# All hyena filter spectra in one opening stage, and the context's convolution behind both latent orders

## The chip, the cores and the metric

The kernel runs on one core of a Trainium2 chip. The metric is device time of one execution, in microseconds (us). The core has five engines with a queue of instructions each: TensorE (PE, matrix multiply, with its weight loads listed as PEld), VectorE (DVE), ScalarE (ACT), GpSimd (POOL) and SyncE (SP). SP and POOL issue the transfers (DMA) between HBM and the on-chip memories, SBUF and PSUM (where matmuls write). Engines wait for each other on semaphores. "Granted clock" is the share of TensorE's full clock that the profile shows: 1.00 is the level of 2.4 GHz, 0.50 that of 1.2 GHz.

## The reference

A two-layer backbone over 1024 latent tokens and 256 context tokens of width 1024. In each layer one input projection feeds three mixers side by side (hyena, retention, latent attention), then come an output projection and an MLP. The change touches the opening and the hyena mixer. A hyena mixer convolves 256 channels twice (two "orders") with a filter as long as the sequence, through Fourier transforms. The filter comes from a small network of the position alone, so its spectrum depends on the layer's weights and the length, and on no token:

```
def hyena_filter_spectrum(L, w1, b1, sin_freq, w2, b2, w3):
    ...
    z = jnp.concatenate([t, jnp.cos(ang), -jnp.sin(ang)], axis=-1)
    h = jnp.sin(sin_freq[0] * (z @ w1 + b1))
    h = jnp.sin(sin_freq[1] * (h @ w2 + b2))
    h = (h @ w3).reshape(L, 2, HY_ORDER, HY_WIDTH)
    ...
    h = h * jnp.exp(-t[:, :, None, None] * deltas)
    fwd, bwd = h[:, 0], h[:, 1]
    kern = jnp.concatenate([(fwd[0] + bwd[0])[None], fwd[1:], jnp.zeros_like(fwd[:1]), bwd[1:][::-1]], axis=0)
    kern = kern / jnp.sum(jnp.abs(kern), axis=0, keepdims=True)
    return jnp.fft.rfft(kern, axis=0)

def long_conv(z, kf, bias):
    ...
    y = jnp.fft.irfft(jnp.fft.rfft(zf, n=2 * L, axis=1) * kf, n=2 * L, axis=1)[:, :L]
    return (y + zf * bias).astype(z.dtype)

def hyena_mixer(u, conv_w, conv_b, w1, b1, sin_freq, w2, b2, w3, bias):
    ...
    u = short_conv(u, conv_w, conv_b)
    x1, x2, v = jnp.split(u, 3, axis=-1)
    ...
    z = x1 * long_conv(v, kf[:, 0], bias[0])
    return x2 * long_conv(z, kf[:, 1], bias[1])
```

The first layer runs the mixer on latent and context tokens, the second on latent tokens only. The modulation of a layer is silu(c) @ w_ada + b_ada for both conditions.

## The kernel before, in words

The program is a chain of blocks; every engine finishes a block before any starts the next. Within a block each engine's instructions run in the order in which the code writes them.

**Opening.** `phase_start` (L158) loads two condition vectors. `phase_ada` (L185) multiplies them with the first third of w_ada in eight chunks of 1 MB ("chunks" below), through a ring of six buffers: 8 matmuls of 256 columns each (L247), two small transposes (L239), a bias add on DVE. SP then loads x (5 MB) and ACT takes its square sums (L155).

**Hyena.** `phase_hyena(kit, l, s)` runs three times: layer 0 latent (s=0), layer 0 context (s=1), layer 1 latent. Each run has:
- a block (L1605) that loads, runs the filter network (two sines, on 64 partitions) and the short convolution of V, and starts the transfer of the transform tables on POOL's queue (L1585, 12 MB for the latent length);
- for each order o a block (L1691) that computes the filter's taps (L1704: full fp32 matmuls with 64 contraction rows), multiplies them with a decay (L1759), splits them into a high and a low part (L1723 on ACT, L1771 on DVE), sums absolute values (L1726, L1773, L1747) for the norm (L1717, L1781, L1782), and turns z by transposes (L1714);
- a block (L1798) that transforms the filter ("K forward": four tiles kt of 48 matmuls of 256 columns), multiplies it by the norm (L1872, L1898 to L1904), transforms z ("z forward", the same size, f0 to f3 below), forms the products of the two for each kt (DVE L1913 to L1925, POOL L1879 to L1885, ACT L1861 to L1865), transforms back (b0 to b3, each 24 matmuls of 512 columns), and computes the outputs (L1930, L1932). DVE also runs the three-tap short convolution of that order's gate there (`conv`, L1590 to L1593). After order 1 SP stores the result (L1806).

Each product of two fp32 matrices is done as three fp32r matmuls (L143 to L145), high×high, high×low, low×high. The stage behind the latest hyena run is the output projection, whose first load on SP (L1990) shows where hyena ended.

Of the kernel before, what the change touches and what calls it, by code (L numbers as in the profile page):

```python
# [19 lines left out]
F32 = mybir.dt.float32  # L20
# [5 lines left out]
P = 128  # L26
# [69 lines left out]
class Kit:  # L96


    def __init__(self, nc, ctx, io):
        self.nc = nc  # L100
        self.ctx = ctx
        self.io = io
        self.base = ((nc.sbuf_base + 31) // 32) * 32
        self.big = self.base + SMALL
        self.signals = {}
        self.placed = {}
# [6 lines left out]
    def sig(self, name, step=1):  # L113
        if name not in self.signals:
            self.signals[name] = Signal(self.nc, self.ctx, name, step)
        return self.signals[name]

# [40 lines left out]
def phase_start(kit):  # L158

    nc, io, s = kit.nc, kit.io, kit  # L160
    loaded = kit.sig("start_loaded", 16)
    loaded.plan(["ident", "c0", "c1"])
    craw = kit.at("craw", [P, 2, KT], 120)
    with nc.Block() as block:
        @block.sync
        def _(sp):
            sp.dma_start(kit.ident[:], io["ident"]).then_inc(loaded.sem, 16)
            sp.dma_start(craw[:, 0, :], io["c"][0].rearrange("(p j) -> p j", j=KT)).then_inc(loaded.sem, 16)
            sp.dma_start(craw[:, 1, :], io["c_ctx"].rearrange("(p j) -> p j", j=KT)).then_inc(loaded.sem, 16)
# [12 lines left out]
ADA_W = 256


def phase_ada(kit):  # L185


    nc, io, ps = kit.nc, kit.io, kit.ps
    n_chunks = 2 * D // ADA_W
    ring = 6  # L190
    w = kit.at("ada_w", [P, ring, KT, ADA_W], 122)
    bias = kit.at("ada_bias", [2, 2 * D], 0)
    row = kit.at("ada_row", [2, 2 * D], 24)
# [6 lines left out]
    w_in = [kit.sig(f"ada_w_in{s}", 16) for s in range(ring)]  # L200
    for s in range(ring):
        w_in[s].plan([c for c in range(n_chunks) if c % ring == s])
    small_in, summed, added = kit.sig("ada_small_in", 16), kit.sig("ada_summed"), kit.sig("ada_added")
    turned, mod_ready = kit.sig("ada_turned"), kit.sig("ada_mod_ready")
    small_in.plan(range(3))
    for s in (summed, added, turned, mod_ready):
        s.plan(range(n_chunks))
    w_dram = io["w_ada"][0].rearrange("(p j) n -> p j n", j=KT)
    with nc.Block() as block:
        @block.sync  # L210
        def _(sp):
            for cond in range(2):
                sp.dma_start(bias[cond:cond + 1, :], io["b_ada"][0:1, 0:2 * D]).then_inc(small_in.sem, 16)
            sp.dma_start(gain[:, :, :], io["norm_g"][0]).then_inc(small_in.sem, 16)
            for c in range(n_chunks):
                if c >= ring:
                    sp.wait_ge(summed.sem, summed[c - ring])
                sp.dma_start(w[:, c % ring, :, :], w_dram[:, :, c * ADA_W:(c + 1) * ADA_W]).then_inc(w_in[c % ring].sem, 16)

            for i in range(2):  # L220
                sp.dma_start(x[:, 4 * i:4 * i + 4, :],
                             io["x"][0, 512 * i:512 * i + 512].rearrange("(t p) n -> p t n", p=P)).then_inc(x_in[i].sem, 16)
            sp.dma_start(x[:, 8:10, :], io["ctx"][0].rearrange("(t p) n -> p t n", p=P)).then_inc(x_in[2].sem, 16)
            for i in range(3):
                sp.wait_ge(x_in[i].sem, x_in[i][0])

        @block.scalar
        def _(act):
            for t in range(ALL_TILES):
                act.wait_ge(x_in[t // 4].sem, x_in[t // 4][0])  # L230
                square_sum(kit, act, squared, t, 4)

        @block.tensor
        def _(pe):
            def turn(c):
                pe.wait_ge(added.sem, added[c])
                for h in range(ADA_W // P):
                    at = c * ADA_W + h * P
                    last = pe.transpose(ps[:, 2 + c % 2, 2 * h:2 * h + 2], row[:, at:at + P], kit.ident[0:2, 0:2])  # L239
                last.then_inc(turned.sem, 1)  # L240

            for c in range(n_chunks):
                pe.wait_ge(w_in[c % ring].sem, w_in[c % ring][c])
                if c >= 2:
                    pe.wait_ge(added.sem, added[c - 2])
                for j in range(KT):
                    last = pe.matmul(ps[0:2, c % 2, 0:ADA_W], kit.cond[:, j, :], w[:, c % ring, j, :],  # L247
                                     start=(j == 0), stop=(j == KT - 1))
                last.then_inc(summed.sem, 1)
                if c:  # L250
                    turn(c - 1)
            turn(n_chunks - 1)

        @block.vector
        def _(dve):
            def mod(c):
                dve.wait_ge(turned.sem, turned[c])
                for h in range(ADA_W // P):
                    t = c * (ADA_W // P) + h
                    last = dve.tensor_copy(kit.mod[:, t, :], ps[:, 2 + c % 2, 2 * h:2 * h + 2])  # L260
                last.then_inc(mod_ready.sem, 1)

            dve.wait_ge(small_in.sem, small_in[2])
            for c in range(n_chunks):
                dve.wait_ge(summed.sem, summed[c])
                cols = slice(c * ADA_W, (c + 1) * ADA_W)
                dve.tensor_tensor(row[:, cols], ps[0:2, c % 2, 0:ADA_W], bias[:, cols], ALU.add).then_inc(added.sem, 1)
                if c:
                    mod(c - 1)
            mod(n_chunks - 1)  # L270
            dve.wait_ge(mod_ready.sem, mod_ready[n_chunks - 1])
            modulation_factor(kit, dve, gain, 0)

# [341 lines left out]
def phase_in(kit, l):  # L615
# [22 lines left out]
    stored = [kit.sig(f"in_stored{s}", 16) for s in range(2)]  # L638
# [904 lines left out]
def phase_hyena(kit, l, s):  # L1543

# [16 lines left out]
    z = kit.at(f"hy_z{s}", [P, 2, length], 160)
    h2 = kit.at(f"hy_h2{s}", [HY_FFN, length], 168)
    w3 = kit.at("hy_w3", [HY_FFN, 2, 2 * W], 172)
    w3_raw = kit.at("hy_w3_raw", [HY_FFN, 4 * W], 176)
    feat = kit.at(f"hy_feat{s}", [HY_EMB, length], 112)
    v_in = kit.at(f"hy_v_in{s}", [P, 2, length + 2], 117)
    w1, w2 = kit.at("hy_w1", [HY_EMB, HY_FFN], 116), kit.at("hy_w2", [HY_FFN, HY_FFN], 116.25)
    cols = kit.at("hy_cols", [HY_FFN, 4], 116.5)
    arg, rnd = kit.at(f"hy_arg{s}", [HY_FFN, length], 96), kit.at(f"hy_rnd{s}", [HY_FFN, length], 100)
    h1 = kit.at(f"hy_h1{s}", [HY_FFN, length], 104)  # L1570
# [3 lines left out]
    xg = kit.at(f"hy_gate{s}", [P, 2, length], 194)  # L1574
    knorm = kit.at("hy_knorm", [P, W], 202)
    decay, ksum = kit.at(f"hy_decay{s}", [P, 2 * K, W], 96), kit.at("hy_ksum", [P, W], 203)
    pmf, pabs = kit.at("hy_pmf", [P, 2, 2, W], 176), kit.at("hy_pabs", [P, 2, 2, W], 184)
    u_in = [kit.at(f"hy_u_in{s}", [P, length + 2], kb) for kb in (104, 188)]
    n_chunk = max(1, length // 512)
    CH = min(512, length)  # L1580

    def tables(pool, which):
        for i in which:
            for a in range(2):
                pool.dma_start(tabs[i][a][:], io[f"hy_tab{s}"][i, a]).then_inc(tab_in.sem, 16)  # L1585

    def conv(dve, out, u, part):

        w = kit.hy_conv[:, part, :]
# [862 lines left out]
```

## Time and profile before

| | us |
|---|---|
| three runs: lowest, median, highest | 4262.32, 4266.14, 4268.31 |
| the profiled execution's span | 4261.7 |
| TensorE busy in it | 3720.1 |
| opening, 0 to 49.9 | 49.9 |
| hyena layer 0, latent, 943.4 to 1198.1 | 254.7 |
| hyena layer 0, context, 1198.1 to 1286.9 | 88.8 |
| hyena layer 1, latent, 3137.2 to 3396.3 | 259.2 |

The span is one execution on the profiler's clock; the runs are timed apart from it. The stages' limits are where SP issues a stage's first transfer, which it can only do when all engines have left the block before. The four stages make up 652.6 us of the span. A row of the timeline gives start and duration in us, engine, line, operation, tiles, count, and in brackets how long the engine sat idle before it and what released it.

### The profile page before, as it was taken

How to read it: one execution, taken by the hardware profiler on the slowest of the kernel's cores; microseconds unless marked ns; L12 is line 12 of the kernel's file. 1: busy time of each engine (PE TensorE's matmuls, PEld its weight loads, DVE VectorE, ACT ScalarE, POOL GpSimd, SP SyncE). 2: the span in 40 equal slices, each digit the busy share in tenths (PEclk: the TensorE clock that was granted, in tenths of full speed). 3: DMA queues.
4: the chain of work that ended last, by engine and by line, in shares of the span. 5: the costliest groups of instructions: out<-in, count | busy, mean ns of one | idle time of the engine just before them, and what ended most of it. 6: DMA issues, size and time to landing. Idle time of an engine off the chain costs nothing. (4 is left out here: it accounts for less than half of the span.)

```text
span 4261.7 us, 54579 instructions
## 1 busy us (share of the span) xinstructions
PE 3720.1 (87%) x20116; PEld 3116.5 (73%) x20116; DVE 2267.7 (53%) x3970; ACT 1415.5 (33%) x2841; POOL 1306.3 (31%) x1182
## 2 busy tenths in 40 slices
PE   6997688877847899999999897698968788999998
PEld 4897577766625688888888697577847767888886
DVE  4853566656663344444444752576766625445454
ACT  3112466651111422222223312466741123222222
POOL 1211011123331155555554211011123313545454
PEclk8998799997868899999999898799978899999999
DMA  5530000012013111111110630000040122111111
GB/s 188 192 110 3 28 1 13 1 54 112 20 43 141 50 40 39 39 39 39 34 35 10 203 121 4 25 1 11 6 157 20 45 95 69 59 39 52 47 49 54
DMA packets 145678, 243.97 MB, mean 57 GB/s; under 512 B 9480, under 2 KB 113689, under 8 KB 141915
## 3 DMA queue, kind: packets, MB, share of 16 engines
q1 hardware_dynamic: 138108, 208.57, 14.8%
q0 software_dynamic: 7392, 33.03, 2.1%
q8 instruction: 111, 1.82, 0.2%
q14 instruction: 67, 0.54, 0.0%
HBM read 215.60 MB, written 25.99 MB: 57 GB/s over the span
## 5 line engine op out<-in xcount | busy, mean ns | idle before, releaser
L2242 POOL TENSOR_TENSOR x<-x,mlp_tmp 128x512 f32<-128x512 f32 x576 | 785.5, 1396 | 805.9 <-DVE mlp_tmp L2223 800.8
L2223 DVE TENSOR_TENSOR mlp_tmp<-psum,gate 128x512 f32<-128x512 f32 x576 | 391.8, 689 | 273.2 <-POOL x L2242 194.6
L143 PE MATMUL psum<-act_hi,w_hi 128*128 128x512 f32 (+1 forms) x1280 | 472.8, 369 | 12.6 <-DVE w_lo L2201 12.6
L144 PE MATMUL psum<-act_lo,w_hi 128*128 128x512 f32 (+1 forms) x1280 | 472.5, 369 | 0.0
L145 PE MATMUL psum<-act_hi,w_lo 128*128 128x512 f32 (+1 forms) x1280 | 472.4, 369 | 0.0
L143 PE MATMUL psum<-w_hi,hidden_hi 128*128 128x512 f32 x1152 | 449.9, 391 | 0.0
L144 PE MATMUL psum<-w_lo,hidden_hi 128*128 128x512 f32 x1152 | 448.4, 389 | 0.0
L145 PE MATMUL psum<-w_hi,hidden_lo 128*128 128x512 f32 x1152 | 448.2, 389 | 0.0
L2215 DVE TENSOR_TENSOR hidden_lo<-square,hidden_hi 128x512 fp32r<-128x512 f32 x160 | 102.4, 640 | 592.6 <-ACT hidden_hi L2187 592.6
L1378 DVE TENSOR_REDUCE att_max<-psum 128x1 f32<-128x512 f32 (+2 forms) x272 | 217.9, 801 | 183.5 <-PE psum L145 183.3
L2179 ACT ACTIVATE relu<-psum 128x512 f32<-128x512 f32 x160 | 88.9, 555 | 666.8 <-PE psum L145 666.8
L143 PEld LDWEIGHTS psum<-act_hi,w_hi 128*128 128x128 f32 x1280 | 242.5, 189 | 54.0 <-DVE w_lo L2201 13.2
L1269 ACT ACTIVATE probs<-psum,att_max 128x512 f32<-128x512 f32 (+2 forms) x272 | 208.7, 772 | 192.4 <-DVE att_max L1382 188.6
L144 PEld LDWEIGHTS psum<-act_lo,w_hi 128*128 128x128 f32 x1280 | 242.4, 189 | 40.8
L145 PEld LDWEIGHTS psum<-act_hi,w_lo 128*128 128x128 f32 x1280 | 242.3, 189 | 40.3
L143 PE MATMUL psum<-w_in_hi,act_hi 128*128 128x256 f32 (+1 forms) x912 | 259.1, 284 | 0.0
L145 PE MATMUL psum<-w_in_hi,act_lo 128*128 128x256 f32 (+1 forms) x912 | 256.7, 282 | 0.0
L144 PE MATMUL psum<-w_in_lo,act_hi 128*128 128x256 f32 (+1 forms) x912 | 256.7, 281 | 0.0
L143 PEld LDWEIGHTS psum<-w_hi,hidden_hi 128*128 128x128 f32 x1152 | 216.3, 188 | 47.7 <-DVE mlp_tmp L2223 3.7
L145 PEld LDWEIGHTS psum<-w_hi,hidden_lo 128*128 128x128 f32 x1152 | 216.3, 188 | 45.2
L144 PEld LDWEIGHTS psum<-w_lo,hidden_hi 128*128 128x128 f32 x1152 | 216.3, 188 | 43.8
L1325 POOL TENSOR_TENSOR att_o_hi<-att_o_hi,att_o_lo 64x256 f32<-64x256 f32 x72 | 52.4, 728 | 604.0 <-ACT att_o_lo L1289 604.0
(325 smaller groups left out, 8608.3 us busy)
## 6 DMA issues: line engine op xcount, KB each, us to landing
w_raw<-in_mlp_w SPq DMA_DIRECT2D x128, 512.0 KB, 3.8
side_w<-in_w_ada SPq DMA_DIRECT2D x40, 1024.0 KB, 6.5
hy_tab<-in_hy_tab POOLq DMA_DIRECT2D x24, 1024.0 KB, 13.6
w_raw<-in_w_in SPq DMA_DIRECT2D x32, 512.0 KB, 4.6
ada_w<-in_w_ada SPq DMA_DIRECT2D x8, 1024.0 KB, 11.5
x<-in_x SPq DMA_DIRECT2D x4, 2048.0 KB, 14.6
wo_raw<-in_w_out SPq DMA_DIRECT2D x16, 512.0 KB, 5.6
hy_scratch<-hy_out POOLq DMA_DIRECT2D x24, 256.0 KB, 3.1
```

The costliest lines, as they stand in the source:

```text
L143: pe.matmul(out, lhs[0], rhs[0], start=start, stop=False)
L144: pe.matmul(out, lhs[0], rhs[1], start=False, stop=False)
L145: return pe.matmul(out, lhs[1], rhs[0], start=False, stop=stop)
L1269: act.activation(pe_[:, n % 2, at:end], psf[:, at:end], ACT.Exp, scale=SCALE, bias=mx[:, n % 2, 1:2], accum_out=sums[:, k, n % SUM_RING:n ...
L1325: kit.pool_chain.link(pool, pool.tensor_tensor(o_hi[rows, :], o_hi[rows, :], o_lo[rows, :], ALU.add))
L1378: dve_last = dve.tensor_reduce(mx[:, n % 2, 6 + k:7 + k], psf[:, at:at + len(part) * P], AX.X, ALU.max)
L2179: act.activation(relu[:, i % 2, 0:n], ps[:, i % 4, 0:n], ACT.Relu).then_inc(relued.sem, 1)
L2215: dve.tensor_tensor(hlo[:, g % 2, f, 0:n], square[:, i % 2, 0:n], hh[:, g % 2, f, 0:n].bitcast(F32), ALU.subtract).then_inc(h_lo.sem, 1)
L2223: dve.tensor_tensor(tmp[:, j % 2, :], ps[:, 4 + j % 4, :], gate[:, int(t >= LAT_TILES), 512 * h:512 * h + 512], ALU.mult).then_inc(gated.s ...
L2242: pool.tensor_tensor(a, a, tmp[:, j % 2, :], ALU.add).then_inc(added.sem, 1)
```

## The change

`phase_open` replaces `phase_start` and `phase_ada`. It runs the filter network for both layers at once (each on 64 of the 128 partitions, all 1280 positions of latent and context in three pieces), its matmuls written between the chunks of w_ada. It then computes taps and spectra in four units (layer l, even or odd taps) of five tiles in layer 0 (four latent, one context) and four in layer 1. A "fold" is one tile's transform for both orders at once: 24 matmuls of 512 columns (6 for context). Between two folds stand the taps of one tile of the next unit, 512 columns twice, for both orders. ACT copies the even fold out of PSUM, DVE adds and subtracts the odd one (`both_parts`), SP writes the sums to a scratch tensor in HBM. The norms are kept in SBUF. The even and odd halves of the tables (8 MB, and 0.5 MB for context) come on POOL's queue. x is loaded before the last unit, and its squares are taken at the end of the block.

`phase_hyena(kit, l)` is one block without filter work. SP loads the rows of V, X1, the context's three parts, and X2 (1 MB each for latent), then each order's spectra, 512 KB for a tile, in two buffers. POOL's queue brings 8 MB of forward tables, a tile at a time, and 4 MB of back tables. The first tap of a short convolution moves to ACT, and X2's convolution stands on DVE between the second and third products of order 0. The norm is applied as ACT's scale on the result of the back transform, a step ahead of the outputs. In layer 0 the context's two orders run behind both latent orders.

The core of the diff:

```
-def phase_start(kit):
-def phase_ada(kit):
+def phase_open(kit):
...
+            def taps(g):
...
+                for c in range(2):
+                    last = pe.matmul(ps[:, 2 * (i % 2) + c, :], h2[rows, place(g)[2]], w3[rows, c, :], start=True, stop=True)
+                last.then_inc(filt.sem, 1)
...
+                for c in range(2):
+                    js = range(K) if s == 0 else [0]
+                    for j in js:
...
+                        last = three_pass(pe, ps[:, 4 + 2 * (n % 2) + c, :], t, [pm[units.index(u) % 2][:, at, a, c, :] for a in range(2)],
+                                          j == 0, j == js[-1])
+                last.then_inc(folded.sem, 1)
...
+            for c in range(3):
+                first(c)
...
+            chunk(0)
+            for c in range(3):
+                second(c)
+                chunk(c + 1)
...
+            for j, g in enumerate(tiles_of[units[0]]):
+                taps(g)
+                if 4 + j < n_chunks:
+                    chunk(4 + j)
             turn(n_chunks - 1)
+            pe.wait_ge(mod_ready.sem, mod_ready[n_chunks - 1])
+            for n, u in enumerate(units):
+                after = tiles_of[units[n + 1]] if n + 1 < len(units) else []
+                for j, f in enumerate(tiles_of[u]):
...
+                    if j == 0:
+                        pe.wait_ge(pm_lo.sem, pm_lo[tiles_of[u][-1]])
+                    fold(f)
+                    if j < len(after):
+                        taps(after[j])
+                for g in after[len(tiles_of[u]):]:
+                    taps(g)
+                if after:
+                    for l, s in norm_after(after[-1]):
+                        norm(l, s, after[-1])
...
+            for kt in range(K):
+                pool.dma_start(tab[0][:, kt, 0:4], io["hy_ahead0"][:, kt, 0:4]).then_inc(tab_in[kt].sem, 16)
+            pool.dma_start(tab[1][:], io["hy_ahead1"]).then_inc(tab1_in.sem, 16)
+            for kt in range(K):
+                pool.dma_start(tab[0][:, kt, 4:8], io["hy_ahead0"][:, kt, 4:8]).then_inc(odd_tab_in.sem, 16)
...
-def phase_hyena(kit, l, s):
+def phase_hyena(kit, l):
...
+            rows((0, V))
+            rows((0, X1))
+            if context_too:
+                for part in (V, X1, X2):
+                    rows((1, part))
+            rows((0, X2))
+            spectrum(steps[0])
+            spectrum(steps[1])
+            for step in steps[2:]:
+                spectrum(step)
...
+            for o in range(2):
+                for m in range(4):
+                    turn(0, o, m)
+                forward(0, o, 0)
+                forward(0, o, 1)
+                forward(0, o, 2)
+                back(0, o, 0)
+                forward(0, o, 3)
+                back(0, o, 1)
+                back(0, o, 2)
+                back(0, o, 3)
+            for o in range(2 if context_too else 0):
+                turn(1, o, 0)
+                forward(1, o, 0)
+                back(1, o, 0)
...
+                act.activation(bank, bank, ACT.Copy, scale=norm).then_inc(scaled.sem, 1)
...
+            products((0, 0, 0))
+            products((0, 0, 1))
+            for ct in range(2):
+                conv((0, X2), ct)
+            products((0, 0, 2))
+            products((0, 0, 3))
+            outputs(0, 0)
...
-            phase_hyena(kit, l, 0)
-            if not last:
-                phase_hyena(kit, l, 1)
+            phase_hyena(kit, l)
```

How the instructions stand in three places follows. First TensorE at the program's start, where the chunks of w_ada (L247 before, L322 after) were alone (before):

```order
L247 MATMUL psum<-ada_w_87,cond 2x256 x16
L239 MATMUL psum<-ident,ada_row_89 128x2 x2
L247 MATMUL psum<-ada_w_87,cond 2x256 x8
```

and after (L310 and L315 are the network's first and second layer, L347 the taps, L152 the first matmul of a fold; `open_tab` are the tables, `open_pm` the split taps):

```order
L310 MATMUL psum<-open_feat_66,open_w_17_76 128x512 x2
L310 MATMUL psum<-open_feat_66,open_w_17_76 128x256
L322 MATMUL psum<-ada_w_71,cond 2x256 x8
L315 MATMUL psum<-open_h_10_69,open_w_18_77 128x512
L322 MATMUL psum<-ada_w_71,cond 2x256 x8
L333 MATMUL psum<-ident,ada_row_75 128x2 x2
...
L347 MATMUL psum<-open_w_21_80,open_h_23_82 128x512 x2
L322 MATMUL psum<-ada_w_71,cond 2x256 x8
...
L333 MATMUL psum<-ident,ada_row_75 128x2 x2
L152 MATMUL psum<-open_pm_5_64,open_tab_0_59 128x512
```

The network's second layer and the taps now stand between the chunks, and the folds behind all of them.

Second, VectorE in the first latent order of layer 0: the two sides of the gate's convolution. Before, it stood ahead of the norm's products (L1898 to L1904) and had three instructions a row tile (`hy_gate` is the convolved gate):

```order
L1590 TENSOR_SCALAR hy_gate_117_11330<-hy_u_in_123_11336,hy_conv 128x1024
L1591 SCALAR_TENSOR_TENSOR hy_gate_117_11330<-hy_u_in_123_11336,hy_conv,hy_gate_117_11330 128x1024
L1593 SCALAR_TENSOR_TENSOR hy_gate_117_11330<-hy_u_in_123_11336,hy_conv,hy_gate_117_11330 128x1024
...
L1898 TENSOR_TENSOR hy_t_113_11326<-psum,hy_knorm_11331 128x512
L1902 TENSOR_TENSOR hy_spec_93_11306<-hy_t_112_11325,hy_t_113_11326 128x512
```

After, X2's convolution stands between the last step of products 1 (L2250, L2251) and the first of products 2 (L2238 to L2240):

```order
L2250 TENSOR_TENSOR hy_uv_111_12351<-hy_t_117_12357,hy_uv_110_12350 128x512
L2251 TENSOR_TENSOR hy_uv_111_12351<-hy_t_118_12358,hy_uv_110_12350 128x512
L2219 SCALAR_TENSOR_TENSOR hy_gate_107_12347<-hy_in_12363,hy_conv,hy_gate_107_12347 128x1024
L2220 SCALAR_TENSOR_TENSOR hy_gate_107_12347<-hy_in_12363,hy_conv,hy_gate_107_12347 128x1024
L2219 SCALAR_TENSOR_TENSOR hy_gate_107_12347<-hy_in_12363,hy_conv,hy_gate_107_12347 128x1024
L2220 SCALAR_TENSOR_TENSOR hy_gate_107_12347<-hy_in_12363,hy_conv,hy_gate_107_12347 128x1024
L2238 TENSOR_TENSOR hy_t_116_12356<-hy_e_12360,psum 128x512
L2239 TENSOR_TENSOR hy_t_116_12356<-hy_e_12360,psum 128x256
```

Third, SP's queue in layer 1's hyena (`hy_scratch` holds the projected rows). Before, network inputs, rows and decays, in blocks of their own:

```order
L1610 DMA hy_feat_104_11317<-in_hy_feat 33x1024
...
L1610 DMA hy_w_raw_11316<-in_hy_ffn_w 64x1024
L1613 DMA hy_v_in_105_11318<-hy_scratch 128x1024 x2
L1605 UNCONDITIONAL_BRANCH
L1692 UNCONDITIONAL_BRANCH
L1694 DMA hy_decay_119_11332<-in_hy_decay 128x2048
L1697 DMA hy_u_in_123_11336<-hy_scratch 128x1024
```

After, all rows first, then eight spectra:

```order
L1986 DMA hy_in_12361<-hy_scratch 128x2x1024
L1986 DMA hy_in_12362<-hy_scratch 128x2x1024
L1986 DMA hy_in_12363<-hy_scratch 128x2x1024
L1996 DMA hy_spec_12349<-spec_scratch 128x4x256 x8
L2296 DMA wo_raw_12403<-in_w_out 128x2x512 x2
L2013 DMA cat_scratch<-hy_z_105_12345 128x1024 x2
```

The spectra (1 KB pieces) stand behind 3 MB of rows on SP, and beside the 12 MB of tables on POOL's queue.

## Rows read from the trace of the kernel before

**Rows 1.** Two stages: length, busy PE, PEld, DVE, ACT, POOL (count), clock, DMA, GB/s.

```profile
0.00:49.90 49.90, 31.79 (x144) 12.21 (x144) 5.04 (x28) 12.13 (x23) 0.41 (x5) 0.96 0.80 275
943.40:1198.10 254.70, 194.21 (x1036) 152.59 (x1036) 166.31 (x218) 44.54 (x75) 85.23 (x91) 0.78 0.20 76
```

**Rows 2.** The timeline of SP: first transfer of stages beside the change.

```profile
49.88 1.47 SPq L607 DMA_DIRECT2D w_raw<-in_w_in  x3
943.40 0.32 SPq L1610 DMA_DIRECT2D hy_feat<-in_hy_feat  x1
1198.09 0.32 SPq L1610 DMA_DIRECT2D hy_feat<-in_hy_feat  x1
1286.93 0.80 SPq L1990 DMA_DIRECT2D cat_raw<-cat_scratch  x2
3137.16 0.32 SPq L1610 DMA_DIRECT2D hy_feat<-in_hy_feat  x1
3396.33 0.80 SPq L1990 DMA_DIRECT2D cat_raw<-cat_scratch  x2
```

**Rows 3.** Four short stretches, columns as in the first group.

```profile
982.00:990.00 8.00, 7.70 (x12) 3.05 (x12) 6.40 (x13) 5.67 (x11) 2.17 (x3) 0.50 1.07 420
1010.00:1015.00 5.00, 5.00 (x44) 5.00 (x44) 2.59 (x4) 0.60 (x1) 1.29 (x1) 1.00 0.00 0
1095.00:1105.00 10.00, 10.00 (x17) 3.83 (x17) 7.98 (x15) 6.07 (x12) 3.31 (x5) 0.50 0.00 1
12.00:20.00 8.00, 8.00 (x30) 2.82 (x29) 0.41 (x1) 0.00 (x0) 0.00 (x0) 1.00 1.08 351
```

**Rows 4.** The timeline: w_ada chunks, one square sum, four taps matmuls.

```profile
11.89 8.76 PE L247 MATMUL psum<-ada_w,cond 128*2 128x256 f32 x32 [11.89 <-DMA ada_w<-in_w_ada]
24.55 3.62 PE L247 MATMUL psum<-ada_w,cond 128*2 128x256 f32 x16
39.21 1.01 ACT L155 ACTIVATE psum<-x 128x1024 f32<-128x1024 f32 x1
982.30 3.78 PE L1704 MATMUL psum<-hy_w,hy_h 64*128 64x512 f32 x4 [1.20 <-DVE hy_pmf L1763]
```

**Rows 5.** The timeline of latent orders, layer 0: transforms, products, outputs.

```profile
1004.03 0.55 PE L143 MATMUL psum<-hy_pm,hy_tab 128*128 128x256 f32 x1 [2.79 <-PEq L1691]
1012.08 0.60 ACT L1855 ACTIVATE hy_t<-psum 128x512 f32<-128x512 f32 x1 [13.65 <-PE psum L145]
1029.36 0.60 ACT L1855 ACTIVATE hy_t<-psum 128x512 f32<-128x512 f32 x1 [5.16 <-PE psum L145]
1035.12 0.60 ACT L1861 ACTIVATE hy_e<-psum 128x512 f32<-128x512 f32 x1 [5.16 <-PE psum L145]
1083.84 0.39 PE L144 MATMUL psum<-hy_tab,hy_uv 128*128 128x512 f32 x1
1084.07 0.39 PE L145 MATMUL psum<-hy_tab,hy_uv 128*128 128x512 f32 x1
1085.64 0.69 DVE L1932 TENSOR_TENSOR hy_z<-hy_t,hy_gate 128x512 f32<-128x512 f32 x1
1194.34 0.69 DVE L1932 TENSOR_TENSOR hy_z<-hy_t,hy_gate 128x512 f32<-128x512 f32 x1
```

**Rows 6.** Groups of instructions, layer 0's latent hyena: busy us, mean ns, idle before.

```profile
L1591 DVE SCALAR_TENSOR_TENSOR hy_gate<-hy_u_in,hy_conv,hy_gate 128x1024 f32<-128x1024 f32 x4 | 5.1, 1283 | 0.1
L1657 DVE SCALAR_TENSOR_TENSOR hy_arg<-hy_rnd,hy_arg 64x1024 f32<-64x1024 f32 x6 | 7.3, 1216 | 0.2
```

**Rows 7.** DMA issues of layer 0's latent hyena: count, KB each, median us to landing.

```profile
hy_tab<-in_hy_tab POOLq DMA_DIRECT2D x12, 1024.0 KB, 13.7
hy_decay<-in_hy_decay SPq DMA_DIRECT2D x2, 1024.0 KB, 4.8
```

**Rows 8.** The timeline of one context order: back transform and last output.

```profile
1243.31 0.47 PE L143 MATMUL psum<-hy_tab,hy_uv 128*128 128x128 f32 x1 [11.94 <-DVE hy_uv L1925]
1249.18 0.29 DVE L1932 TENSOR_TENSOR hy_z<-hy_t,hy_gate 128x128 f32<-128x128 f32 x1
```

More of the change, by code:

```diff
@@ L105, in __init__ @@
         self.signals = {}
+        self.retired = []
         self.placed = {}
@@ L196, in phase_ada @@
     x_in = [kit.sig(f"proj_raw{i}", 16) for i in range(3)]
-    for i in range(3):
-        x_in[i].plan([0])
+    for s in x_in:
+        s.plan([0])
     squared.plan(range(ALL_TILES))
[L200 to L204, printed above, removed]
@@ L205, in phase_ada, with taps_at, norm_after, sums_of @@
-    small_in.plan(range(3))
-    for s in (summed, added, turned, mod_ready):
-        s.plan(range(n_chunks))
+    odd_folds = [f for f in folds if f[0][1] == 1]
+    def taps_at(g):
+        return ps[:, 2 * (G[g] % 2):2 * (G[g] % 2) + 2, :]
+    def norm_after(g):
+        if g == ((0, 1), K):
+            return [(0, 0), (0, 1)]
+        return [(1, 0)] if g == ((1, 1), K - 1) else []
+    def sums_of(l, s):
+        return ksum if s == 0 else ksum_ctx
     w_dram = io["w_ada"][0].rearrange("(p j) n -> p j n", j=KT)
@@ L220, in _ @@
-            for i in range(2):
[L221 to L231, printed above, removed]
+                if c >= RING:
+                    sp.wait_ge(chunk_sum.sem, chunk_sum[c - RING])
@@ L233, in _ @@
+            for i in range(2):
+                sp.wait_ge(spec_sent[i].sem, spec_sent[i].total)
+            for s in x_in:
+                sp.wait_ge(s.sem, s[0])
         @block.tensor
         def _(pe):
[L235 to L240, printed above, removed]
@@ L242, in _, with first, second @@
-            for c in range(n_chunks):
-                pe.wait_ge(w_in[c % ring].sem, w_in[c % ring][c])
+            def first(c):
+                c0, c1 = MLP_CHUNKS[c]
+                pe.matmul(ps[:, c, 0:c1 - c0], w1[0:HY_EMB, :], feat[0:HY_EMB, c0:c1], start=True, stop=True).then_inc(first_sum.sem, 1)
+            def second(c):
+                c0, c1 = MLP_CHUNKS[c]
+                pe.wait_ge(sined.sem, sined[(0, c)])
+                pe.matmul(ps[:, c, 0:c1 - c0], w2[:], h1[:, c0:c1], start=True, stop=True).then_inc(second_sum.sem, 1)
@@ L244, in _, with chunk @@
+            def chunk(c):
+                pe.wait_ge(w_in[c % RING].sem, w_in[c % RING][c])
                 if c >= 2:
@@ new lines, in norm @@
+            def norm(l, s, g):
+                bank = 2 * ((G[g] + 1) % 2)
+                pe.wait_ge(ksummed.sem, ksummed[g])
+                pe.wait_ge(pm_lo.sem, pm_lo[gens[G[g] - 1]])
+                pe.wait_ge(absed.sem, absed[gens[G[g] - 1]])
+                for i in range(4):
+                    last = pe.matmul(ps[:, bank + s, i:i + 1], sums_of(l, s)[:, i * P:(i + 1) * P], kit.ones[:, 0:1],
+                                     start=True, stop=True)
+                last.then_inc(norm_sum.sem, 1)
@@ L261, in mod @@
-                last.then_inc(mod_ready.sem, 1)
-            dve.wait_ge(small_in.sem, small_in[2])
[L264 to L269, printed above, removed]
+                t = c * (ADA_W // P)
+                dve.tensor_copy(kit.mod[:, t:t + 2, :],
+                                ps[:, 6 + c % 2, 0:4].rearrange("p (a b) -> p a b", a=2)).then_inc(mod_ready.sem, 1)
@@ L1573, in phase_hyena @@
     e_sb = kit.at("hy_e", [P, 2, W], 192)
[L1574 to L1585, printed above, removed]
@@ new lines, in phase_hyena @@
+    for o in range(2 if context_too else 0):
+        uses += [("turn", 1, o, 0), ("ahead", 1, o, 0), ("back", 1, o, 0)]
+    U = {use: n for n, use in enumerate(uses)}
+    invs = [(ct, par) for par in range(2) for ct in range(2)]
+    got = {key: kit.sig(f"hy_got{i}", 16) for i, key in enumerate(u_in)}
+    for sg in got.values():
+        sg.plan(range(1))
+    halo, conv_begun, conved = kit.sig("hy_halo"), kit.sig("hy_conv_begun"), kit.sig("hy_conved")
+    halo.plan(range(1))
+    convs = [(0, V), (0, X1)] + ([(1, V), (1, X1), (1, X2)] if context_too else []) + [(0, X2)]
@@ L1936, in out_first_loads @@
+            products((0, 0, 3))
+            outputs(0, 0)
+            for m in range(4):
+                turn_lo(0, 1, m)
+            for kt in range(4):
+                products((0, 1, kt))
+            outputs(0, 1)
+            for o in range(2 if context_too else 0):
+                turn_lo(1, o, 0)
+                products((1, o, 0))
+                outputs(1, o)
 def out_first_loads(kit, l, sp):
```

991 lines of the change are left out of this document (626 added, 365 removed).

## The prediction

> **What bounds the kernel now.** I read the stages' limits first, in SP's timeline. Hyena takes 1286.93 − 943.40 = 343.5 us in layer 0 and 3396.33 − 3137.16 = 259.2 us in layer 1; the opening takes 49.9 [rows 2]. The rest of the program is not edited. Then the engines by stage: in layer 0's latent hyena TensorE is busy for 194 of 254.7 us at a mean clock of 0.78, VectorE for 166, and no engine is full [rows 1]. So this is a chain, not a throughput: each block ends with its last engine, and the next starts with an idle TensorE. In the opening TensorE (31.8 of 49.9 us) follows the arrival of the w_ada chunks, at 275 GB/s [rows 1].
>
> Two levels of the clock matter. With fp32r transforms back to back it is 1.00, and 0.50 in the taps stretches, although TensorE is busy there for 10.00 of 10.00 us [rows 3]. Transfers reach 420 GB/s where tables dominate and 351 where only 1 KB pieces of w_ada come [rows 3].
>
> **What one latent order costs without its filter.** Transforms of z begin as ACT picks up the filter's last tile, at 1029.36, and the last output ends at 1085.64 + 0.69 = 1086.3: 57 us [rows 5]. The 12,288 columns of one tile's transform take 1035.12 − 1029.36 = 5.76 us at full clock; the first after idling took 1012.08 − 1004.03 = 8.05, so a cold start costs 2.3 [rows 5].
>
> **Layer 1 after, from the block's start.**
> - V lands. A 1 MB transfer beside the tables lands in 4.8 us in the median [rows 7]; with issue, 6.
> - Convolution of V: first tap on ACT (1.0 [rows 4]), then four DVE passes of 1.28 [rows 6], the first ready at 7: to 12.3. X1, behind it on DVE, 5.1: 17.4. Then four low parts of the turned z (0.7 each, half of the 1024-column pass of [rows 6]), 2.7: 20.2. The transposes and ACT's copies run under X1.
> - Order 0: 57, plus 2.3 cold, plus X2's convolution (4 × 1.28 = 5.1), which stands on DVE with products 2 and 3 queued behind it, and b2, b3 waiting for these. DVE is busy for 166 of the stage's 254.7 us [rows 1], so a part may fall into idle time, but products 2 and 3 come one behind the other with no slack that I can show, so I count it whole. ACT's scale adds 0.6: 85.2.
> - Turning z for order 1: transposes and ACT's first copy 0.9, then four low parts of 0.7: 3.7. Order 1: 2.3 + 57 + 0.6: 148.8.
> - Store and block end: 1198.09 − (1194.34 + 0.69) = 3.1 [rows 2, 5]. **152** against 259.2: **−107**.
>
> Tables: 12 MB on POOL's queue plus 4 MB on SP's by then are 16.8 million bytes, 40 us at 420 GB/s [rows 3]. b0 starts behind f0 to f2 at 20.2 + 8.05 + 2 × 5.76 = 40. They just fit, so I cost the tables at nothing; this cover is thin.
>
> **Layer 0 after.** The same 148.8, then the context behind it. One context order is a turn (2.3), a transform of 12 matmuls at half clock (2.6) with ACT's copy (0.6), the product chain, in which TensorE idles for 11.94, and from the back transform's start to the last output 1249.18 + 0.29 − 1243.31 = 6.2 [rows 8], plus 1 for the scale: 24.6. The two are serial, nothing else being left to run: 49. With the store, 3.1: **201**, against 343.5: **−142**.
>
> **Opening after.** It now carries the filter work of all three runs.
> - To the first fold. Inputs land at about 6. The first sine is about seven DVE passes over 1280 positions, up to 1.2 us for 1024 [rows 6], the shorter ones nearer 0.7: 9.7. The first chunk, at 11.89 before [rows 4], shares the transfer engines with 8.5 MB of tables: 18, plus up to 5.4 for a cold chunk. The second sine stands on DVE with bias adds between its pieces; TensorE takes its last piece at 37. Five taps and four chunks follow in turn. Four old taps matmuls took 3.78 at half clock [rows 4], one new tile is the same amount; a chunk takes 3.6 [rows 4] to 5.4. At full clock this is 5 × 1.9 + 4 × 3.7 = 24, at half 40; with 4.5 for the last tile's split it ends at 66 to 81. I take 71. The last chunk can't come before 19.4 million bytes (8 + 8.5 + 2 MB) at 420 GB/s, 46, which lies under this.
> - Folds: 24 × 0.23 [rows 5] = 5.5; sixteen and two of 1.4: 91.
> - Taps between folds: 13 × 1.9 = 24 at full clock, with the split on DVE and ACT under the next fold (three DVE passes against 7.4 us of TensorE).
> - Between units the first fold waits for the last tile's split: a DVE pass (1.2), two ACT passes (1.0 each), a DVE pass (1.2), 4.5 with hand-overs; in two of the three cases the norm, which TensorE does first, adds the sum on POOL and matmuls, about 4 each: 22. Each wait costs a cold start, 2.3: 7.
> - Tail: last fold, DVE's sums 2.5, store 3, end: 6.
>
> 71 + 91 + 24 + 22 + 7 + 6 = **221**, against 49.9: **+171**. Loading x and its ten squares (1.0 each [rows 4]) lie under the last unit (22 us).
>
> **Sum.** +171 − 107 − 142 = −78 against the profiled span of 4261.7: 4184. The runs' median stands 4.4 above that span: **4188**. So of 249 us that hyena gives up, two thirds come back in the opening. TensorE's transforms of the filters are the same columns as before; what goes is waiting.
>
> **Where a price was chosen.** The opening's 221 has ends of 195 (taps at full clock, unit waits half covered by the context folds) and 245 (half clock in the taps, 16 more in the transfers).
>
> **Rivals.**
> *B, transfers crowd each other.* The chunks of w_ada and the spectra come in 1 KB pieces, beside tables in 8 KB and larger ones; the decay, in 8 KB rows, got about its half (4.8 us for 1 MB, about 210 GB/s) [rows 7], but small pieces beside tables are not in any row. If they get an eighth, the first chunk lands at about 26 (+8), chunks then come at 3 us each (351 GB/s [rows 3]), and the opening pays 8 to 25; in each latent stage the first spectra land some 12 late, with the product chain of both engines waiting. Together +33, 4221; at most 4240. For it: w_ada alone already ran at 351 rather than 420. The Trainium skill, "DMA: Bandwidth & Descriptors", section "Queues, rings and completion order", says that each transfer engine takes turns between queues by whole packets, not by bytes. By that rule queues of unlike packet sizes do not share bytes equally, which speaks for B and against this change; the decay's row neither shows nor excludes it.
> *C, the waits are better covered.* The opening takes 195 and each latent stage 5 less, X2's convolution lying in DVE's idle time: 4188 − 26 − 10 = 4152. For it: DVE is idle for 88 us of the old stage [rows 1]. Against it: each wait is by itself longer than the context's 1.4.
> *D, slower: TensorE stays at half clock in the folds.* The taps were the only work seen at 100% busy and 0.50 [rows 3], and now thirteen taps stand between the folds. If they hold the clock down through the folds, folds cost 91 and taps 24 more: +115, 4303. It decides from about two thirds of that on (78). Against it: pure fp32r work ran at 1.00 [rows 3], and folds outlast taps three to one. The Trainium skill, "TensorE: Matmul & The Clock Gate", Part 1, says that the throttle is the default and that sustained activity lifts it. The busy row at 0.50 disagrees, so I don't lean on the rule against D.
> *E, no gain:* some 45 of D's 115 together with B's 33, within 0.2% of before.
>
> **Chances.** Forecast (4165 to 4215) 0.58; B 0.17; C 0.15; D 0.06; E 0.04. A measurement of this kernel tells about 0.2% (8.5 us) from no change. Faster holds the forecast, B and C: 0.90; same 0.04; slower 0.06. The range 4155 to 4240 takes in the forecast, B and about half of C, and leaves out some 2 in 10.
>
> **What the profile after would show.** The first load of w_in on SP at about 221; hyena 201 and 152 long; granted clock 0.9 or more in the folds (D wrong), with dips at the three unit changes; TensorE waiting there for DVE's low parts; chunk 0 at 18 (B: 26); no wait of the products for spectra and b0 not waiting for the back table (B: both wait); DVE busy without a gap from products 1 over X2's convolution to products 2. I am wrong if the opening is far from 221, the only stage whose work has no like row, or if the transfers, which were idle for most of hyena, become what the products wait for.

## The result, and the profile after

The changed kernel takes 4227.76 us (median of 4 runs, 4226.42 to 4232.78) against 4265.12 before: a ratio of 0.9918, 95% interval 0.9903 to 0.9932. It is faster by 37, not by 78. Its profiled execution has a span of 4224.8, 36.9 below that of before. The timeline of SP, with the same stage limits as [rows 2]:

```profile
242.40 1.49 SPq L951 DMA_DIRECT2D w_raw<-in_w_in  x3
1141.33 0.89 SPq L1986 DMA_DIRECT2D hy_in<-hy_scratch  x2
1353.55 9.01 SPq L2345 DMA_DIRECT2D cat_raw<-cat_scratch  x4
3197.66 1.40 SPq L1986 DMA_DIRECT2D hy_in<-hy_scratch  x3
3358.64 8.27 SPq L2345 DMA_DIRECT2D cat_raw<-cat_scratch  x4
```

| us | before | forecast | after |
|---|---|---|---|
| opening | 49.9 | 221 | 242.4 |
| layer 0's hyena | 343.5 | 201 | 212.2 |
| layer 1's hyena | 259.2 | 152 | 161.0 |
| the three | 652.6 | 574 | 615.6 |

All three are longer than forecast, by 21, 11 and 9, and their sum, 37.0 below before, is the whole difference. The stages between them, which the change doesn't edit, differ by up to 8 from one execution to the next, one way or the other; so single executions are compared below by stage.

**The opening.** TensorE's timeline (the network's first layer, the first chunk of w_ada, the first fold):

```profile
12.04 4.63 PE L310 MATMUL psum<-open_feat,open_w 33*128 33x512 f32 x6 [12.04 <-DMA open_w_raw<-in_hy_w]
35.54 5.50 PE L322 MATMUL psum<-ada_w,cond 128*2 128x256 f32 x16 [18.87 <-DMA ada_w<-in_w_ada]
87.87 0.80 PE L152 MATMUL psum<-open_pm,open_tab 128*128 128x512 f32 x1 [7.87 <-DVE mod L518]
```

TensorE stands for 18.87 us before chunk 0, which lands at 35.5, not 18. From there to the first fold it is 52 us; the forecast had 53. So all of that term's error is the chunk. The stretches from 10 to 35.5 us (the last two columns are the transfer engines' busy share and GB/s) show the transfer engines full meanwhile:

```profile
10.00:20.00 10.00, 4.63 (x6) 1.83 (x6) 6.87 (x12) 0.73 (x2) 0.00 (x0) 1.00 1.19 414
20.00:30.00 10.00, 0.00 (x0) 0.00 (x0) 5.26 (x12) 1.05 (x2) 0.00 (x0) 1.00 1.06 414
30.00:35.50 5.50, 0.00 (x0) 0.00 (x0) 0.00 (x0) 0.00 (x0) 0.00 (x0) 1.00 1.07 355
```

414 is near the rate of the tables in [rows 3], 355 near the 351 of the chunks: the chunks come when the tables are done, at about 30. What SP's queue got until then shows in the packets of the two queues (packets, MB, share of 16 engines; q0 is POOL's queue, q1 is SP's), from 12 to 19 us, 19 to 25 and 30 to 35.5:

```profile
q0 software_dynamic: 460, 2.84, 103.3%
q1 hardware_dynamic: 460, 0.06, 18.3%
q0 software_dynamic: 203, 1.43, 59.8%
q1 hardware_dynamic: 208, 1.05, 47.4%
q1 hardware_dynamic: 1724, 1.75, 97.2%
q0 software_dynamic: 40, 0.20, 9.4%
```

While both have work, the queues take turns packet for packet (460 and 460, 203 and 208), whatever the packets hold. From 12 to 19 us that costs most: there SP's queue is at the identity matrix, the condition vectors and the biases, and its 460 packets hold only 0.06 MB, against 2.84 MB of tables. The decay behind them, in 8 KB pieces, then gets nearly half. Chunk 0 stands behind both; when SP's queue comes to its 1 KB pieces, hardly any table packets are left.

**Layer 1's hyena.** VectorE and ScalarE: X1's rows, the first products.

```profile
3202.69 2.37 ACT L2114 ACTIVATE hy_z<-hy_in,hy_conv 128x1024 f32<-128x1024 f32 x2 [9.70 <-DMA hy_in<-hy_scratch]
3213.15 2.37 ACT L2114 ACTIVATE hy_gate<-hy_in,hy_conv 128x1024 f32<-128x1024 f32 x2 [8.09 <-DMA hy_in<-hy_scratch]
3231.09 0.69 DVE L2238 TENSOR_TENSOR hy_t<-hy_e,psum 128x512 f32<-128x512 f32 x1 [9.15 <-ACT hy_e L2131]
3240.21 1.23 DVE L2243 TENSOR_TENSOR hy_t<-hy_t,hy_spec 128x1024 f32<-128x1024 f32 x1 [7.77 <-DMA hy_spec<-spec_scratch]
```

V's 1 MB lands 5 us into the block, X1's 10.5 later. The first product, ready at 3232.4, waits 7.77 for its spectrum, 42.5 us into the block. In layer 0 ScalarE waits for the context's rows, ahead of its copy for the first products:

```profile
1168.85 1.09 ACT L2114 ACTIVATE hy_gate<-hy_in_ctx,hy_conv 128x256 f32<-128x256 f32 x2 [8.81 <-DMA hy_in_ctx<-hy_scratch]
1182.99 1.09 ACT L2114 ACTIVATE hy_gate<-hy_in_ctx,hy_conv 128x256 f32<-128x256 f32 x2 [13.04 <-DMA hy_in_ctx<-hy_scratch]
```

That is the forecast's rival B, at a higher price. Rival D fell: with taps and chunks, then with taps and folds, the clock held the level of 2.4 GHz (at a unit change it dipped, as the forecast had it; run 4 shows the rows):

```profile
50.00:66.00 16.00, 15.95 (x67) 6.10 (x64) 9.96 (x21) 4.01 (x5) 0.18 (x1) 1.00 0.30 95
150.00:200.00 50.00, 46.76 (x174) 31.50 (x173) 27.95 (x32) 15.04 (x16) 6.99 (x6) 1.00 0.26 105
```

### The profile page after: what moved, and what is told of

Its sections match the earlier page's. It is cut to its first block and busy times, and to the rows that moved or that the text cites. A ratio compares the mean times of both kernels' runs of the same rounds, so it can differ in the third digit from the quotient of the medians.

```text
span 4224.8 us, 53466 instructions
## 1 busy us (share of the span) xinstructions
PE 3677.8 (87%) x19724; PEld 3089.1 (73%) x19724; DVE 2203.1 (52%) x3828; ACT 1434.6 (34%) x2836; POOL 1265.3 (30%) x1107
## 5 line engine op out<-in xcount | busy, mean ns | idle before, releaser
L152 PE MATMUL psum<-act_hi,w_hi 128*128 128x512 f32 (+1 forms) x1280 | 472.3, 369 | 12.9 <-DVE w_lo L2556 12.9
L152 PE MATMUL psum<-w_hi,hidden_hi 128*128 128x512 f32 x1152 | 449.8, 390 | 0.0
L1722 DVE TENSOR_REDUCE att_max<-psum 128x1 f32<-128x512 f32 (+2 forms) x272 | 217.8, 801 | 179.7 <-PE psum L154 179.6
L152 PEld LDWEIGHTS psum<-act_hi,w_hi 128*128 128x128 f32 x1280 | 242.0, 189 | 54.3 <-DVE w_lo L2556 13.5
L153 PEld LDWEIGHTS psum<-act_lo,w_hi 128*128 128x128 f32 x1280 | 242.1, 189 | 40.7
L154 PEld LDWEIGHTS psum<-act_hi,w_lo 128*128 128x128 f32 x1280 | 242.0, 189 | 40.2
L152 PE MATMUL psum<-w_in_hi,act_hi 128*128 128x256 f32 (+1 forms) x912 | 259.1, 284 | 0.0
L152 PEld LDWEIGHTS psum<-w_hi,hidden_hi 128*128 128x128 f32 x1152 | 216.3, 188 | 47.6 <-DVE mlp_tmp L2578 3.6
```

What stands on the lines that cost most here:

```text
L152: pe.matmul(out, lhs[0], rhs[0], start=start, stop=False)
L153: pe.matmul(out, lhs[0], rhs[1], start=False, stop=False)
L154: return pe.matmul(out, lhs[1], rhs[0], start=False, stop=stop)
L1722: dve_last = dve.tensor_reduce(mx[:, n % 2, 6 + k:7 + k], psf[:, at:at + len(part) * P], AX.X, ALU.max)
```

## The experiments

The theory: beside tables in pieces of 8 to 32 KB, transfers in small pieces get a share by the size of their pieces, so what is issued beside the tables comes when these end. The rivals: place in the queue and the sum of bytes alone; or TensorE's and VectorE's own chain. Stage lengths (us) of each run's profile, read as above, and the run's time (median of timed runs, or the one run):

| run | opening | layer 0 | layer 1 | time |
|---|---|---|---|---|
| changed kernel | 242.4 | 212.2 | 161.0 | 4227.8 |
| tables behind the chunks | 224.0 | 211.7 | 161.0 | 4206.1 |
| spectra first | 242.1 | 217.8 | 157.1 | 4223.5 |
| spectra in 4 KB pieces | 241.5 | 213.7 | 154.3 | 4221.6 |
| norm behind the fold | 241.2 | 212.3 | 161.0 | 4228.2 |
| tables in 2 KB pieces | 237.8 | 212.4 | 161.0 | 4224.7 |
| tables behind the rows | 242.4 | 194.6 | 147.4 | 4194.9 |
| convolutions moved | 241.6 | 195.9 | 143.3 | 4189.3 |
| all together | 220.8 | 197.7 | 143.5 | 4172.0 |
| first table early | 220.6 | 198.3 | 143.5 | 4173.1 |

**1. Tables behind the chunks** (opening).

```
+            pool.wait_ge(w_in[1].sem, w_in[1][n_chunks - 1])
             for kt in range(K):
                 pool.dma_start(tab[0][:, kt, 0:4], io["hy_ahead0"][:, kt, 0:4]).then_inc(tab_in[kt].sem, 16)
```

> One line added in the opening: POOL waits for the last chunk of w_ada before it issues the tables. Theory 1, the tables crowd out the chunks (1 KB pieces beside 8 KB and larger): chunk 0 lands at about 10 instead of 35.5, the second sine starts when the first has ended, the folds start at 60 to 66 instead of 87.9, and the opening ends at 215 to 222 instead of 242.4. Theory 2, TensorE and VectorE set the pace to the first fold whatever the transfers do: the folds start no earlier than 82, the opening stays at 237 or above. Theory 3, the total of 19.5 MB at 420 GB/s sets it: the last table lands as late as the last chunk did, the folds wait for tables, and the gain is below 10.

The median of four executions is 0.9868 of before (0.9851 to 0.9885). TensorE's timeline:

```profile
16.96 5.83 PE L322 MATMUL psum<-ada_w,cond 128*2 128x256 f32 x16 [6.24 <-DMA ada_w<-in_w_ada]
69.63 0.80 PE L152 MATMUL psum<-open_pm,open_tab 128*128 128x512 f32 x1 [7.88 <-DVE mod L519]
```

Chunk 0 lands 18.6 earlier, the first fold starts 18.2 earlier, the opening ends 18.4 earlier. Theory 1 holds, but its figures were too good: chunk 0 came 7 later than it said, the folds 4 to 10 and the opening's end 2 to 9, since chunk 0 still stands behind w3 and the decay (in run 8 the decay goes behind chunk 3, and chunk 0 lands at 12.35). Theories 2 and 3 fall.

**2. Spectra first**, and ACT's tap of X2 behind the second products (hyena).

```
             rows((0, X1))
+            spectrum(steps[0])
+            spectrum(steps[1])
...
             rows((0, X2))
-            spectrum(steps[0])
-            spectrum(steps[1])
```

> In the hyena block SP loads the first two spectra ahead of the context's rows and X2; ACT's tap of X2 moves behind the second products, so that X2 may come late. Theory 1 (what waits is the transfer queued last on SP): in layer 1 the products no longer wait for the spectrum (7.8 us before), X2's convolution waits about 1 for ACT; layer 1's hyena 154 to 156 instead of 161.0. In layer 0 the context's rows now come last and still stand ahead of the first products on ACT: 211 to 215 instead of 212.2. Theory 2 (the first products are late for another reason, such as the 3 us of ACT's copies): layer 1 stays at 160 to 162.

Layer 1 gains 3.8, not 5 to 7; layer 0 loses 5.6. ScalarE and VectorE in layer 1, from the block's start at 3198.03:

```profile
3213.53 2.37 ACT L2114 ACTIVATE hy_gate<-hy_in,hy_conv 128x1024 f32<-128x1024 f32 x2 [8.09 <-DMA hy_in<-hy_scratch]
3238.26 1.23 DVE L2244 TENSOR_TENSOR hy_t<-hy_t,hy_spec 128x1024 f32<-128x1024 f32 x1 [5.49 <-DMA hy_spec<-spec_scratch]
```

The spectrum is now next behind X1 on SP, and still lands 24.7 us after it: 524,288 bytes at 21 GB/s, at first beside tables in 16 KB pieces, at the end beside the back table's 32 KB pieces. Queue order alone is not the cause.

**3. Spectra in 4 KB pieces**, queue order as in the changed kernel. The scratch tensor gets an order dimension in front, and a read becomes contiguous:

```
-                src = kit.spec_dram[s][l if s == 0 else 0, :, kt].rearrange("p i (c o w) -> p (i c) o w", c=2, o=2)[:, :, o, :]
+                src = kit.spec_dram[s][l if s == 0 else 0, :, kt, o].rearrange("p i c w -> p (i c w)")
```

> The scratch tensor holds each order's spectrum side by side, so that a spectrum is read in pieces of 4 KB instead of 1 KB; the order on SP is unchanged (the writes in the opening are in 1 KB pieces instead of 4 KB, two transfers for one). Theory 1 (a transfer's share beside the tables goes by the size of its pieces): the first spectrum lands at 30 to 35 from the block's start instead of 42.5, the wait of 7.8 shrinks to 0 to 2, layer 1's hyena takes 153 to 156. Theory 2 (only the place in the queue and the sum of bytes count): it lands at 42 as before, 160 to 162. Layer 0 waits for the context's rows first, so it gains at most 2. The opening's end may be 0 to 2 later.

Layer 1 gains 6.6, layer 0 nothing (it is 1.4 longer), and the wait falls from 7.77 to 1.04 (VectorE, block from 3199.53):

```profile
3235.33 1.23 DVE L2244 TENSOR_TENSOR hy_t<-hy_t,hy_spec 128x1024 f32<-128x1024 f32 x1 [1.04 <-DMA hy_spec<-spec_scratch]
```

The same bytes behind 3 MB of rows now land earlier (35.8) than those right behind X1 in 1 KB pieces (40.2). That separates piece size from place. X1, in 4 KB pieces, moved 1 MB in 10.5 us, 100 GB/s beside tables in 16 KB pieces, 4.8 times the rate of run 2's 1 KB pieces. The packets of the changed kernel, from 3203 to 3213 us (X1's 4 KB pieces beside 16 KB) and from 3226 to 3232 (the spectrum's 1 KB pieces beside 16 and 32 KB), are one for one again:

```profile
q0 software_dynamic: 224, 3.41, 81.3%
q1 hardware_dynamic: 224, 0.85, 22.6%
q0 software_dynamic: 97, 2.39, 93.6%
q1 hardware_dynamic: 100, 0.10, 6.0%
```

The Trainium skill, "DMA: Bandwidth & Descriptors", section "Queues, rings and completion order", says that an engine takes turns between queues by packets; the rates and the packet counts agree with it.

**4. Norm behind the fold** (opening).

```
                     fold(f)
+                    if j == 0 and n:
+                        for l, s in norm_after(tiles_of[u][-1]):
+                            norm(l, s, tiles_of[u][-1])
...
-                if after:
-                    for l, s in norm_after(after[-1]):
-                        norm(l, s, after[-1])
```

> In the opening the norm's sums on TensorE move behind the first fold of the next unit, so that this fold no longer stands behind POOL's sum. Theory 1 (TensorE's waits of 8.1 and 6.6 for POOL are on the path, as the forecast counted them at 4 each beyond the split): the folds of units 1 and 3 start 3 to 6 earlier each, the opening ends at 232 to 237 instead of 242.4. Theory 2 (the taps behind the norm then wait as long, or VectorE's sums set the pace): 240 or above.

The opening gains 1.2, so theory 1 falls, though unit 1's first fold does start earlier, at 129.6 against 136.2. The stretches from there, granted clock third from the end:

```profile
128.00:136.00 8.00, 6.37 (x20) 5.10 (x21) 1.82 (x2) 0.20 (x1) 1.28 (x1) 0.65 0.00 0
136.00:144.00 8.00, 7.66 (x31) 5.15 (x30) 2.64 (x7) 0.20 (x1) 0.00 (x0) 0.78 0.01 2
144.00:152.00 8.00, 8.00 (x25) 5.26 (x23) 3.80 (x5) 1.73 (x2) 0.61 (x1) 0.79 0.33 131
```

The same stretches of the changed kernel, where TensorE waits out the unit change until 132.80:

```profile
128.00:136.00 8.00, 3.20 (x15) 3.20 (x16) 2.16 (x4) 1.48 (x2) 1.26 (x1) 0.51 0.00 0
136.00:144.00 8.00, 8.00 (x25) 6.41 (x26) 0.34 (x2) 0.00 (x0) 0.00 (x0) 0.64 0.01 2
144.00:152.00 8.00, 8.00 (x31) 5.26 (x29) 5.31 (x7) 1.94 (x2) 0.00 (x0) 1.00 0.21 83
```

In the run the norm's sums and taps stand between two folds, and the second fold falls back to the level of 1.2 GHz: its first matmuls are 0.43 apart, not 0.23. So a lead of 6.6 at unit 1's first fold is 4.6 at the second and 2.1 at the third. What exactly lowered the clock was not tried, and the way from 2.1 to the 1.2 at the end was not traced.

**5. Tables in 2 KB pieces** (opening): each transfer split in four, one for each table.

```
-                pool.dma_start(tab[0][:, kt, 0:4], io["hy_ahead0"][:, kt, 0:4]).then_inc(tab_in[kt].sem, 16)
+                for a in range(4):
+                    pool.dma_start(tab[0][:, kt, a], io["hy_ahead0"][:, kt, a]).then_inc(tab_in[kt].sem, 16)
...
```

> In the opening the same tables go in the same place on POOL's queue, but each transfer of 1 MB in 8 KB pieces becomes four of 256 KB in 2 KB pieces. Theory 1 (a transfer's share goes by the size of its pieces): the chunks of w_ada and the decay keep a third of the engines instead of a ninth; w3 lands before 10 instead of 12.0, the decay well before 24, chunk 0 at 20 to 26 instead of 35.5, the first fold starts 8 to 14 earlier, the opening ends at 228 to 235. Theory 2 (the sum of bytes ahead on both queues counts): chunk 0 at 34 to 37, the opening at 240 to 244. Should the 36 issues on POOL (0.57 each, 20 us) hold the tables back, the rate would fall below 400 GB/s in the first 20 us.

```profile
7.68 4.63 PE L310 MATMUL psum<-open_feat,open_w 33*128 33x512 f32 x6 [7.68 <-DMA open_w_raw<-in_hy_w]
24.40 5.31 PE L322 MATMUL psum<-ada_w,cond 128*2 128x256 f32 x16 [12.09 <-DMA ada_w<-in_w_ada]
32.82 3.62 PE L322 MATMUL psum<-ada_w,cond 128*2 128x256 f32 x16 [2.04 <-DMA ada_w<-in_w_ada]
40.88 5.30 PE L322 MATMUL psum<-ada_w,cond 128*2 128x256 f32 x16 [3.18 <-DMA ada_w<-in_w_ada]
```

With no other change in order, w3 lands at 7.7 and chunk 0 at 24.4, as theory 1 had it. The opening gains only 4.6, below its 7 to 14: chunks 1 and 2 are now late instead, since the tables still take their part of the bytes. From 26 to 32 us the queues moved 778 and 775 packets, 1.41 MB of tables and 0.78 of chunks. The total fell as well, to 377 GB/s from 10 to 20 us (414 in the changed kernel), below the 400 named; since it was 370 from 20 to 30 too, after POOL's last issue at 19.2, slow issues alone don't explain it. Share goes by piece, and the sum of bytes is the floor under it.

**6. Tables behind the rows** (hyena, with the 4 KB spectra): spectra ahead of X2, and

```
+            pool.wait_ge(ks_in[1].sem, ks_in[1][steps[1]])
             pool.dma_start(ahead[0][:, 0], io["hy_ahead0"][:, 0]).then_inc(tab_in[0].sem, 16)
```

> Hyena, on top of the spectra in 4 KB pieces: SP loads the first two spectra ahead of X2, and POOL waits for the second before it issues the tables. Theory 1: V, X1, the context's rows and the spectra land within 8 to 12 of the block's start, X1's convolution follows V's without a gap, the transforms of z start at 18 to 19 instead of 24.3 and nothing waits for a spectrum or a context row: layer 1's hyena 146 to 150 (161.0), layer 0's 192 to 200 (212.2). Rival: 12 MB of tables that start 8 to 10 later then hold the transforms back (the first table lands at 14, the back table at 40 to 42): layer 1 stays at 153 or above.

147.4 and 194.6, both inside theory 1. (Three edits are in this: of layer 1's 13.6 against the changed kernel, the 4 KB spectra alone gave 6.6.) Of TensorE's waits in layer 1 for transfers only this is left (waits: total, times, longest):

```profile
PE psum L152 <- DMA hy_back<-in_hy_back: 6.9, 1, 6.9
```

**7. Convolutions moved** (on top): X1's behind the turn of z, X2's behind that of order 1, on ACT and DVE.

```
+            for m in range(4):
+                turn_lo(0, 0, m)
             for ct in range(2):
                 conv((0, X1), ct)
-            for m in range(4):
-                turn_lo(0, 0, m)
...
```

> On top of that, X1's convolution moves behind the turn of z, so that it runs while TensorE does the first transform, and X2's convolution behind the turn of order 1. If X2's 5.1 in the middle of order 0 and X1's 5.1 ahead of the transforms lie on the path, as the forecast had them, layer 1's hyena is 9 to 11 shorter than in the run before it, 136 to 140; layer 0's 5 to 10 shorter, since there the context's convolutions (5.8 on VectorE) then reach past the first transform. If they were hidden, no change.

Layer 1 gains 4.1 of the 9 to 11, layer 0 loses 1.3. The last output of order 0 in layer 1, in run 6 and here:

```profile
3263.03 0.69 DVE L2263 TENSOR_TENSOR hy_z<-psum,hy_gate 128x512 f32<-128x512 f32 x1
3256.59 0.69 DVE L2263 TENSOR_TENSOR hy_z<-psum,hy_gate 128x512 f32<-128x512 f32 x1
```

It ends 78.0 into the block instead of 83.6. X1's move gives 0.6 of these 5.6, since the first transform now waits for its table; X2's convolution cost the other 4.9 there, and order 1 takes it in for 1.5. In layer 0, order 0 gains only 0.6, with TensorE waiting 5.2 for the first table and 9.3 for the back table, and order 1 costs 2.9 more. TensorE's waits in layer 1:

```profile
PE psum L152 <- DMA hy_back<-in_hy_back: 7.2, 1, 7.2
PE psum L152 <- DMA hy_ahead<-in_hy_ahead: 2.9, 1, 2.9
```

**8. All together**, with the decay behind chunk 3 in the opening.

> All of it together: tables behind the last chunk in the opening, the decay behind chunk 3 there, and the hyena of the run before. Stages add up if they are independent: opening 220 to 224 (chunk 0 some 3 earlier than with the tables behind alone), layer 0's hyena 183 to 192, layer 1's 136 to 140, so 70 below the changed kernel, 4150 to 4165.

The median of five executions is 4171.97, 0.9784 of before (0.9771 to 0.9797): 91 below the runs of before beside it, and some 56 below the changed kernel. The opening, 220.8, is as expected; the two hyena stages, 197.7 and 143.5, are not (183 to 192 and 136 to 140), for the reason in 7, and so the time misses 4150 to 4165.

**9. First table early:** its issue moves ahead of the wait.

> As the run with all of it together, but POOL issues the first forward table (2 MB) before it waits for the second spectrum. Theory (the first transform waits for this table, 2.9 in layer 1 and 5.2 in layer 0 in the run before, because the tables start late): these waits go, since V lands first on its queue and X1 is not wanted before the turn of z; layer 1's hyena 139 to 142 instead of 143.5, layer 0's 191 to 195 instead of 197.7, the median 4160 to 4168. Rival (the table crowds out X1 and the spectra, the stage is as long or longer): 4172 or above.

No change: 0.9785 (0.9769 to 0.9802). TensorE's wait for the first table is gone, and that for the back table in layer 1 is 10.2 instead (in run 8 the two were 2.8 and 8.0):

```profile
PE psum L152 <- DMA hy_back<-in_hy_back: 10.2, 1, 10.2
```

The rival's number came, not by its mechanism: in layer 1 the wait moved from the first table to the last. That the 12 MB of tables and what goes before them are now the bound fits this; other orders were not tried.

## Why the prediction was wrong

- **What failed: "shares the transfer engines with 8.5 MB of tables: 18".** It took the decay's half of the bytes, which 8 KB pieces get beside 8 KB pieces [rows 7], for a queue whose pieces are mostly smaller. Packets go one for one, so small pieces ahead of chunk 0 took the 7 us from 12 to 19 for 0.06 MB, and SP's queue came to chunk 0 itself only when the tables were nearly done. It landed at 35.5, and 17 of the opening's 21 are that; run 1 gives 18.4 back. The floor by bytes, 46, was beside the point: the first chunk counted, not the last.
- **"They just fit, so I cost the tables at nothing"** failed in the same way. The tables were not late; they made V's followers late. The last outputs of order 0 and order 1 in layer 1, then in layer 0:

```profile
3294.12 0.69 DVE L2261 TENSOR_TENSOR hy_z<-psum,hy_gate 128x512 f32<-128x512 f32 x1
3354.88 0.69 DVE L2261 TENSOR_TENSOR hy_z<-psum,hy_gate 128x512 f32<-128x512 f32 x1
1241.98 0.69 DVE L2261 TENSOR_TENSOR hy_z<-psum,hy_gate 128x512 f32<-128x512 f32 x1
1301.19 0.69 DVE L2261 TENSOR_TENSOR hy_z<-psum,hy_gate 128x512 f32<-128x512 f32 x1
```

Order 0 ended 97.2 into layer 1's block, 12 later than the forecast's 85.2, with X1 and the spectrum late, and 101.3 into layer 0's, 16 later, with the context's rows (1 KB pieces) late. The stages are only 9 and 11 over because order 1 was forecast too long: 63.6 against 60.8 and 59.2, an error the other way, whose cause was not traced. That, in the main, is why run 6 gives back more than the 9 and 11, namely 13.6 and 17.6.
- Rival B had the mechanism and a price of 33, against 41 for all three stages together: it had chunk 0 at 26, and left out the context's rows. That 4228 still lies between 4155 and 4240 is because the range took in B, not because the sum held. B's 0.17 was too low: no row showed small pieces beside tables, and the forecast took the favourable end.
- **Right:** X2's convolution on the path of order 0 (5.1 forecast, 4.9 measured, of which 1.5 comes back when it moves to order 1), the context's tail with store and end (52, against 1353.55 − 1301.88 = 51.7, from the last latent output), folds, taps and unit waits (150, against 242.4 − 87.9 = 154.5), and D's exclusion. The unit waits are there, but run 4 could not take them away.
- Not tried: what share of the 4 us left in the folds is cold clock, and whether the context's two orders could run inside the latent ones.

## What to carry to other kernels

When transfers move to a stage's start, list them by piece size and not only by bytes: small pieces that are wanted first go ahead of bulk in large pieces, with a wait, or are laid out in larger ones. Ask of the first piece needed and of all that is queued ahead of it, not of the last byte. Here, once that order was right, moving one more issue (run 9) only moved the wait from one table to another.

## What the runs showed of the hardware

- Two queues with work took turns packet for packet: 460 and 460 packets from 12 to 19 us of the changed kernel (2.84 and 0.06 MB), 224 and 224 from 3203 to 3213 (3.41 and 0.85 MB).
- Beside tables in 16 KB pieces and larger, a transfer in 1 KB pieces moved at 21 GB/s (run 2), one in 4 KB pieces at 100 GB/s (the changed kernel); alone, 1 KB pieces move at 351 [rows 3].
- Taps with 64 contraction rows ran at a granted clock of 1.00 between chunks and folds, where they had 0.50 in the old stage [rows 3].
- In run 4, sixteen matmuls of one column and a tile's taps between two folds went with a return to 0.50 in the second fold, although TensorE was busy for 7.66 of the 8 us from 136 to 144; what in them did it was not tried.
